# Attention with the scores one tile ahead, the two heads half a round apart, and merges and output weights in pieces between the last recurrence chains

## What is computed

```python
xn = rmsnorm(h, norm1_g[l]); proj = xn @ w_in[l]
q, k, v, xr, gr, g_merge = jnp.split(proj, splits, axis=-1)
s = jnp.einsum('bqhgd,bkhd->bhgqk', qb, k) * scale
p = jax.nn.softmax(s, axis=-1); attn = jnp.einsum('bhgqk,bkhd->bqhgd', p, v)
xc = centred_dwconv(xr, conv_w[l], conv_b[l])
rnn = rg_lru(xc, ..., False) + rg_lru(xc, ..., True)
rnn = rnn * jax.nn.gelu(gr)
gates = jax.nn.sigmoid(g_merge); mix = g_attn * attn + g_rnn * rnn
h = h + mix @ w_out[l]
hn = rmsnorm(h, norm2_g[l]); gu = hn @ w_ffn_in[l]
h = h + (jax.nn.silu(g) * u) @ w_ffn_out[l]
```

## Time and profile before

| | us |
|---|---|
| median of 3 runs (2319.83 to 2328.8) | 2322.12 |
| the profiled execution, its time | 2322.02 |
| the profiled execution, its span | 2320.2 |

### The profile page before, as it was taken

The page is one execution under the profiler, slowest core; times in us unless marked ns, Lnnn a source line. Parts: engine busy times, 40 slices in busy tenths (PEclk is TensorE's granted clock), DMA queues, the critical chain, the costliest instruction groups (busy, mean ns, idle before and its releaser), DMA issues.

```text
span 2320.2 us, 24316 instructions
## 1 busy us (share of the span) xinstructions
PE 2067.3 (89%) x10160; PEld 1519.7 (65%) x10160; DVE 960.5 (41%) x1371; ACT 637.1 (27%) x960; POOL 469.8 (20%) x319
## 2 busy tenths in 40 slices
PE   5999898999998979888788879888787878999999
PEld 4879787888887763333333337667665666888787
DVE  6864454432333561111111126754544794222343
ACT  3442332321323201000000014343134753222221
POOL 4532132232322511111111020211002240000021
PEclk8899899999999979999899989999999999999999
DMA  4661231221324368999999964201111133323220
GB/s 154 214 175 52 55 89 39 37 73 37 73 37 148 132 239 318 409 411 403 411 412 406 422 271 162 73 22 61 46 46 46 37 109 109 109 73 109 73 91 37
DMA packets 97514, 360.77 MB, mean 155 GB/s; under 512 B 9834, under 2 KB 34572, under 8 KB 85112
## 3 DMA queue, kind: packets, MB, share of 16 engines
q1 hardware_dynamic: 81856, 330.50, 39.6%
q0 software_dynamic: 8240, 19.00, 2.4%
q10 hardware_dynamic: 7304, 9.66, 1.3%
HBM read 338.41 MB, written 29.10 MB: 158 GB/s over the span
## 4 chain that ended last, share of the span: by engine, by line
PE 75%; DVE 12%; ACT 5%; issue 5%; POOL 1%; ACTq 1%; DMA 1%; PEld 0%; SPq 0%; PEldq 0%; DVEq 0%; POOLq 0%
PE ps L269 72%; PE ps L273 3%; DVE H L259 1%; ACT ST L265 1%; ACT L265 1%; DVE ST L253 1%; DVE BG L253 1%; ACT M L266 1%; DVE sm L2894 1%; DVE WL L253 1%; ACT M L265 1%; DVE M L256 1%; POOL WL L253 1%; DVE M L253 0%; DVE ST L2816 0%
## 5 line engine op out<-in xcount | busy, mean ns | idle before, releaser
L269 PE MATMUL ps<-W,BG 128*64 128x512 f32 x672 | 202.6, 647 | 34.6 <-issue 34.6
L269 PE MATMUL ps<-XH,WS 128*128 128x512 f32 x704 | 217.7, 390 | 0.0
L269 PE MATMUL ps<-HTH,WL 128*128 128x512 f32 x448 | 183.1, 409 | 0.0
L269 PEld LDWEIGHTS ps<-ST 128*128 128x128 f32 x1376 | 168.9, 193 | 8.8 <-POOL ST L253 1.7
L269 PE MATMUL ps<-ST 128*128 128x64 f32 (+1 forms) x1376 | 169.0, 275 | 1.2 <-POOL ST L253 1.0
L269 PEld LDWEIGHTS ps<-XH,WS 128*128 128x128 f32 x704 | 132.8, 189 | 27.7
L2094 DVE COPY BG<-ps 128x512 f32<-128x512 f32 x32 | 22.1, 691 | 298.4 <-PE ps L269 298.4
L269 PE MATMUL ps<-XL,WS 128*128 128x512 f32 x352 | 137.6, 391 | 7.7 <-DVE XL L253 7.7
L269 PEld LDWEIGHTS ps<-W,BG 128*64 128x64 f32 x672 | 62.6, 148 | 124.6 <-issue 123.4
L263 ACT ACTIVATE BG<-ps 128x512 f32<-128x512 f32 x48 | 28.5, 595 | 379.2 <-PE ps L273 346.4
L269 PE MATMUL ps<-X2H,GV 128*128 128x512 f32 (+1 forms) x512 | 131.5, 348 | 0.0
(11 more groups left out here) (386 smaller groups left out, 4389.3 us busy)
## 6 DMA issues: line engine op xcount, KB each, us to landing
W<-in_w SPq DMA_DIRECT2D x42, 2048.0 KB, 27.3
W<-in_w_in SPq DMA_DIRECT2D x27, 2048.0 KB, 14.0
ST<-in_w SPq DMA_DIRECT2D x14, 2048.0 KB, 26.2
U<-in_w SPq DMA_DIRECT2D x14, 2048.0 KB, 26.6
M<-in_w SPq DMA_DIRECT2D x13, 2048.0 KB, 27.2
HT<-in_w SPq DMA_DIRECT2D x13, 2048.0 KB, 27.4
W<-in_w_ffn_in SPq DMA_DIRECT2D x22, 1024.0 KB, 7.6
ypad<-BG SPq DMA_DIRECT2D x23, 512.0 KB, 15.0
```

Of the source, the lines that this page charges most:

```text
L269: return p.e.matmul(o, lhsT=l, rhs=r, start=start, stop=stop, skip_group_check=True)
```

## The change

In attention a head's job has five steps. At step i it issues the scores of tile i and then the transposes of tile i-1 (if no pair is in the list, transposes first). The odd head takes its step half a round after the even one. DVE's part is cut in three: `largest`, `divided`, `taken`. The rate of `back` is 0.92 instead of 1.15. In the recurrence `s_rnn` waits for the scans of block n-2 (`scan_done`) where it waited for `rfin_done`, and the merges are collected in `f.due` and issued in an odd block after its DVE operation ahead of the square roots. Output weights: three parts of half 0 whole by DVE after the last granule split; the other 13 parts have their high part from ACT and their low part from DVE, in a list WO_PARTS, three of them at a time between the last chains; POOL no longer takes part. In `v_out` the normalising product goes from DVE to ACT (`s_normed3`), and the first split of the feed-forward weights goes ahead of the output additions. Unused semaphores go. The diff, cut to its core:

```diff
+        WO_PARTS = [(1, 0), (1, 1), (1, 2), (0, 3), (0, 4), (0, 5), (1, 3), (1, 4), (1, 5), (0, 6), (0, 7), (1, 6), (1, 7)]
+        def v_wo_first():
             v.wait_ge(*w_ready[N_OUT])
             v.wait_ge(*B["rg", 7, 3].full())
-            for k in range(k0, k1):
+            for k in range(3):
...
+        def s_wo_high(i, j):
+            for y, k in WO_PARTS[i:j]:
+                s.wait_ge(*w_ready[N_OUT + y])
+                s.wait_ge(*B["s", 7].full())
+                act(WOH[y][:, k, :], weights3(N_OUT + y)[:, k, :], ACT.Copy).then_inc(wo_hi)
+        def v_wo_low(i, j):
+            for n in range(i, j):
+                y, k = WO_PARTS[n]
+                v.wait_ge(wo_hi, n + 1)
+                tt(v, WOL[y][:, k, :], weights3(N_OUT + y)[:, k, :], WOH[y][:, k, :].bitcast(F32), SUB).then_inc(wo_lo[y])
         def v_second(f):
             for j, (kind, n) in GRAN3:
                 if j < len(GRAN) - 1:
                     v_granule(j + 1)
+                if j == len(GRAN) - 2:
+                    v_wo_first()
...
                 elif kind == "s":
-                    if n == 5:
-                        v_wo2(0, 5)
                     f.mul_s[n] = True
                     if f.mul_r[n]:
-                        v_merge2(n)
+                        f.due.append(n)
...
         def p_attn(h, f, singles, pairs):
-            for i in range(NT):
+            last = None
+            for i in range(NT + 1):
+                if j:
+                    yield
+                first = i < NT and bool(pairs)
+                x = scores(i) if first else None
+                if i:
+                    turned(i - 1, *last)
+                if i < NT and not first:
+                    x = scores(i)
+                last = x
+                yield
+                if not j:
+                    yield
...
         def v_attn(h, f):
+            for i in range(NT + 1):
+                if j:
+                    if i:
+                        divided(i - 1)
+                    yield
+                if i < NT:
+                    largest(i)
+                if i:
+                    taken(i - 1)
+                yield
+                if not j:
+                    if i < NT:
+                        divided(i)
+                    yield
...
         def s_rnn(n, f):
             if n > 1:
-                s.wait_ge(rfin_done, n - 1)
+                s.wait_ge(scan_done, 2 * n - 2)
...
             s.wait_ge(c8_done, 1)
+            if n > 1:
+                s.wait_ge(rfin_done, n - 1)
...
         def v_rnn(n, f):
                 stt(z, z, 1.0, th, ADD, MUL).then_inc(rq_done)
-            yield
-            yield
+            if n % 2:
+                v_merges(f)
+            yield
+            yield
+            if n > 5:
+                v_wo_low(3 * (n - 6), 3 * (n - 5))
...
             weave([lambda n=n: v_rnn(n, f) for n in range(8)], 2, back, 1.25)
+            v_wo_low(6, 9)
+            v_merges(f)
+            v_wo_low(9, 13)
...
         def v_out():
-            v_wo2(5, 8)
+            v_split_in(0)
             v_added(0)
             v_added(1)
-            v_normed(0)
+            v_rms3(0)
...
         def s_out():
-            s_wo2()
+            s_wo_high(3, 13)
             s.wait_ge(mx_done, 8)
+            s_split_in(0)
             s_squared(0)
             s_squared(1)
+            s_normed3(0)
```

More of the change, by code:

```diff
@@ L2852, in p_attn, with scores @@
             pt = pts[j]
-            for i in range(NT):
+            def scores(i):
                 b = pairs.pop(0)
@@ L2886, in v_attn, with largest @@
         def v_attn(h, f):
[L2887 to L2891, removed]
+            j, mine = h % 2, []
+            def largest(i):
+                t, mxc = B["sc", h, i], mxs[:, 4 * (h % 4) + i:4 * (h % 4) + i + 1]
+                mine.append(pbs[len(f.pb) % 3])
                 f.pb.append((h, i))
@@ L2914, in s_attn @@
             j = h % 2
[L2915 to L2923, removed]
+            for i in range(NT + 1):
+                if j:
+                    yield
+                if i:
+                    s.wait_ge(*B["pT", h, i - 1].full())
+                    t = B["sc", h, i - 1]
+                    act(pts[j][0:16, 4, (i - 1) * P:i * P], t.at[0:16, 896:1024], ACT.Copy).then_inc(t.drained)
+                if i < NT:
+                    col, c = 4 * (h % 4) + i, len(f.pb)
+                    pb = pbs[c % 3]
+                    f.pb.append((h, i))
+                    s.wait_ge(max_done[j], 4 * (h // 2) + i + 1)
+                    if c > 2:
+                        s.wait_ge(*B[("pT",) + f.pb[c - 3]].full())
+                    act(pb, wide(B["sc", h, i]), ACT.Exp, bias=mxs[:, col:col + 1], accum=sms[:, col:col + 1]).then_inc(exp_done[j])
                 yield
-                s.wait_ge(*B["pT", h, i].full())
-                act(pts[j][0:16, 4, i * P:(i + 1) * P], t.at[0:16, 896:1024], ACT.Copy).then_inc(t.drained)
-                yield
+                if not j:
+                    yield
             while f.out <= at_gran["a", h]:
@@ L2931, in g_attn @@
         def g_attn(h, f):
-            for i in range(2 * NT):
+            for i in range(2 * NT + 2):
                 yield
@@ L3028, in g_rnn, with v_merges @@
             f.mul_r[n] = True
+        def v_merges(f):
+            for m in f.due:
+                v_merge2(m)
+            f.due = []
         def v_rnn(n, f):
@@ L3079, in p_middle @@
             weave([lambda n=n: p_rope(n, f, pairs) for n in range(10)], 4, back, 2.0, drain=False)
-            weave([lambda h=h: p_attn(h, f, singles, pairs) for h in range(8)], 2, upto(f, back, N_GELU + 4), 1.15)
+            weave([lambda h=h: p_attn(h, f, singles, pairs) for h in range(8)], 2, upto(f, back, N_GELU + 4), 0.92)
             weave([lambda n=n: p_rnn(n, f, pairs) for n in range(8)], 2, back, 1.25)
@@ L3096, in s_middle @@
             weave([lambda n=n: s_rope(n, f) for n in range(10)], 4, back, 2.0, drain=False)
-            weave([lambda h=h: s_attn(h, f) for h in range(8)], 2, upto(f, back, N_GELU + 4), 1.15)
+            weave([lambda h=h: s_attn(h, f) for h in range(8)], 2, upto(f, back, N_GELU + 4), 0.92)
             weave([lambda n=n: s_rnn(n, f) for n in range(8)], 2, back, 1.25)
@@ L3103, in g_middle @@
             weave([lambda n=n: g_rope(n, f) for n in range(10)], 4, back, 2.0, drain=False)
-            weave([lambda h=h: g_attn(h, f) for h in range(8)], 2, upto(f, back, N_GELU + 4), 1.15)
+            weave([lambda h=h: g_attn(h, f) for h in range(8)], 2, upto(f, back, N_GELU + 4), 0.92)
             weave([lambda n=n: g_rnn(n, f) for n in range(8)], 2, back, 1.25)
```

65 lines of the change are left out of this document (32 added, 33 removed).

## The result

The changed kernel took 2300.22 us (median of 4 runs, 2297.08 to 2303.06) where the kernel before, run beside it, took 2323.89 (4 runs); the ratio is 0.9902, interval 0.9884 to 0.992. The change makes the kernel 23.7 us faster. The profiled execution took 2298.31 us, with a span of 2296.5.

The account below looks back on a forecast made before the run. TensorE, busy nearly everywhere, was taken as the bound, with 79 us of waits plus clock losses to gain; 2322.0 - 11 (attention) - 8 (recurrence) - 8 (end) - 0.5 (norm) = 2294.5 us, range 2281 to 2311.

Parts of the forecast that it names:

- Attention: All attention stretches together: -7 + 12 - 8.5 - 7.5 = -11 us.
- the recurrence and the end: Recurrence: sigmoids wait for scans, not merges, -8 us; end: the wait before granule `s7` and its low clock go, -8.
- Heads 0 and 1: Attention beside `a` granules: waits for probabilities go, with part of a low clock spell; -7 us.
- Heads 2 to 5 beside `x`: Attention beside `x` granules: a loss, +6 us of idle time and +6 of low clock, +12.
- the five waits: Beside `x` granules: scores wait about 3.3 us for the convolution; four waits taken to bring low spells costing 1.9 each.
- Heads 4 to 7 beside `r`, and 6 and 7 alone: Late attention: transposes stop waiting behind gelu, -8.5 us; VectorE stops waiting for exponentials in heads 6 and 7, -7.5.
- Rival (d): Attention gives nothing, the recurrence and end gains stay: 2309 us, or 2313 with half the recurrence; chance 0.12.
- (b): Attention's `x` granules are no loss, and attention gives 20 to 25 us: 2282 us; chance 0.15.
- net -2.4 for a round: Recurrence: sigmoids 4.1 us sooner, 1.6 come back by merges; a new split wait of about 4.6 us each round.
- Rival (c): Recurrence: a new wait replaces the one removed, merges standing ahead of a granule's split; stage gives 0, 2303 us; chance 0.20.
- The end: Before the output product: the 6.11 us wait of `s7` goes with its low clock spell; -8 us.
- The norm: At the end: the 7.74 us wait for XL shifts and does not shrink; -0.5 us.

Follow-up runs that it names:

- experiment 1: The bank edit: changed kernel with the output product's first two tiles on single banks 1 and 0, not 0 and 1; 2293.71 us, 0.9867 of before.
- experiment 2: Changed kernel, but ScalarE copies each x granule beside attention to SBUF and the convolution reads the copy; 2290.89 us, 0.9848 of before.
- experiment 6: Changed kernel with the output product's first two banks exchanged, and the granules' rate back at 1.15 from 0.92; 2302.91 us, 0.9919 of before.
- experiment 3: Changed kernel with attention, including the granules' rate, as before the change; recurrence and end as changed; 2310.04 us, 0.9933 of before.
- experiment 5: Changed kernel with the output product's first two banks exchanged, and output weights handled as before the change; merges as changed; 2299.11 us, 0.9896 of before.
- experiment 4: Changed kernel with the recurrence's merges at once behind each convolution and ScalarE waiting for them, as before the change; 2310.82 us, 0.9936 of before.
- experiment 8: Changed kernel with first output banks exchanged, x granules copied to SBUF, and merges moved behind the next granule's gate split; 2280.28 us, 0.9825 of before.

## Why the prediction was right, and where it was not

The forecast was 2294.5, and 2300.2 was measured. One wait was missed altogether; without it (experiment 1) the kernel takes 2293.7. That this is so near is in part luck. The terms are made for the stretches, and there 27.5 us were forecast; the changed kernel gains 20.3, and with the bank edit 29.2. Attention gave 3 more than forecast, the recurrence and the end, even with the bank edit, 2 less.

**Heads 0 and 1**: -7 forecast, -7.8 measured; no wait for probabilities is left, and the clock is at 1.00.

**Heads 2 to 5 beside `x`**: +12 forecast, +9.9 measured, with the five waits at the places named. Their cause is shown by experiment 2. The round from 1592.68 to 1606.26 takes 13.6 us where 13.2 was forecast. But the halves of the term don't hold as well as their sum. Idle time rose by 3.9 (18.1 to 22.0), not 6. Matmul time rose by 6.1 where 6 was forecast, but only in part by the clock that the forecast charged. The scores in this stretch (count, busy time, mean ns of one), before and changed:

```profile
L269 PE MATMUL ps<-M,BG 128*128 128x264 f32 x48 | 11.6, 385 | 0.0
L269 PE MATMUL ps<-M,BG 128*128 128x264 f32 x56 | 18.5, 459 | 19.3 <-DVE H L259 13.7 <-DVE ST L259 3.3 <-ACT ST L263 2.2
```

Two tiles' scores more stand in it, because of the order and the rate: 1.9 us by the earlier trace rows, and the stretch behind has as many fewer (48 records before, 40 now). The clock took some 2.5 more than before (0.04 of 114.5 us against 0.02 of 104.6), not 6, and the other 1.7 I can't place. So +12 came near by work that the term didn't count. But the spells were not where I put them. Windows of the changed kernel from about the end of each of the five waits on:

```profile
1592.00:1598.00 6.00, 4.87 (x35) 4.42 (x36) 3.72 (x6) 1.94 (x4) 0.00 (x0) 1.00 0.00 0
1606.00:1612.00 6.00, 5.29 (x38) 4.70 (x38) 2.07 (x5) 1.94 (x4) 1.99 (x1) 1.00 0.00 1
1619.00:1625.00 6.00, 4.71 (x34) 4.26 (x35) 3.87 (x6) 1.94 (x4) 0.00 (x0) 1.00 0.01 3
1655.00:1661.00 6.00, 5.02 (x18) 3.36 (x18) 3.35 (x8) 0.94 (x3) 0.00 (x0) 0.72 0.60 229
1672.00:1678.00 6.00, 5.14 (x18) 4.18 (x19) 3.91 (x8) 0.94 (x3) 0.00 (x0) 0.72 0.01 3
```

Three waits of 3.33 us have no low spell behind them, two have one of 3.4 us ((1.00 - 0.72) x 2 x 6). I had taken four of five.

**Heads 4 to 7 beside `r`, and 6 and 7 alone**: -8.5 and -7.5, together -16; measured -16.6, at a clock of 1.00 over the whole stretch where it was 0.91. Of this 1.9 are the scores that moved ahead of `r0`. The forecast put the gain down to the order alone; by experiment 6 it needs the rate too, since with the old one the new order gains next to nothing from `x0` on (190.7 us, before 191.1).

**Attention** as a whole: -11 forecast, -14.2 measured (233.6 to 219.4); experiment 3 gives 12.6 of them back. Rival (d) falls; (b) too, but experiment 2 shows that its 12 us were there to be had.

**The recurrence and the end**: -8 and -8 forecast. With the bank edit the stretch falls from 128.2 to 114.1, -14.1: merges alone, by experiment 5 against before, -7.3, the pieces on top of them -6.9. So both sizes held, but not as two terms of their own: the pieces without the merges (experiment 4, less 2.7 to 3.8 for the bank) are 0.1 to 1.2 us slower than before, because a merge then stands in the way of the split of `s7`. The step "net -2.4 for a round", with a new wait of about 4.6 us, came as 4.50 and 3.15; its working, which charged the new wait against the gain, is doubtful, since experiment 8 takes the wait away and gains nothing. Rival (c) named the right wait and the wrong price.

**The step that failed** is in "The end": "it costs nothing elsewhere if the ten remaining low parts keep ahead of the output product". They did, and TensorE didn't wait for WL. The output product waited for the bank that `s7` had used, and so for a sigmoid behind three copies that the change put ahead of it. I had followed the list of pairs through the new order, and not the list of singles to its end. Its size is 7.0 us in this stretch, of which -16 was forecast and -7.2 came, and 1.7 behind it by the clock.

**The norm**: -0.5 forecast. The wait for XL is 5.03 where it was 7.74, and the stretch from the output product is +1.1, which is the clock behind the bank's wait; with the bank edit it is 0.7 shorter than before.

## What to carry to other kernels

A change of order has to be followed through every list of buffers to its last user, not only where it was made: here attention gained 14 us, and nearly 9 of them were lost 120 us later, because two banks left the stage exchanged. Where a granule shares buffers with work that needs them next, a copy of 0.6 us for each on an engine with room was worth 12.7 us against four operations out of the accumulators. And a long wait with a clear releaser isn't yet the bound: take it away by itself before it is given a price. When two stretches trade work, as those before and behind `r0` do here, only their sum can be compared.

## What was not expected of the hardware

Some of VectorE's operations take two and a half to nearly four times as long while GpSimd adds or multiplies from SBUF. In the rows of experiment 5 a cast takes 0.42 us ahead of GpSimd's products and 1.55 beside them, a two-input operation 0.69 and 1.71; the product ends at 1867.04, and the cast of twice the size that starts at 1867.50 takes 0.68, where in experiment 4 it took 1.78 beside one. The Trainium skill ("SBUF — State Buffer", section "Who interferes with whom") says that a cast in a two-port mode contends with GpSimd, and a two-input operation with both inputs in SBUF with GpSimd's reads; the trace agrees in that both are slowed, and doesn't show the mode of the cast. The prediction took "up to twice" from it, and the two-input operation is slowed 2.5 times here. The second of the five parts took 1.07 us (1858.02 to 1859.09), so five at that speed are 5.3; together they took 10.5 (from 1856.96 to 1867.50). Part of what the pieces give may come from there; this was not tried apart.

The length of a wait doesn't tell here whether the clock falls behind it: three of 3.33 us left it at 1.00, two of 3.75 and 3.32 were followed by 3.4 us at the lower level, and in the changed kernel a spell also stands between 1579 and 1591, where the waits are 0.90 and 0.79:

```profile
1579.00:1585.00 6.00, 4.31 (x26) 3.35 (x24) 2.73 (x6) 2.67 (x6) 2.34 (x1) 0.91 0.00 0
1585.00:1591.00 6.00, 4.35 (x26) 4.04 (x24) 3.44 (x6) 0.79 (x2) 0.00 (x0) 0.80 0.00 0
```
